# Order of the decode loads and steps: the first four value sequences before the last two key sequences, and three prompt units moved beside the last keys

## The chip, the cores and the metric

One core of one Trainium2 chip runs the whole program. The metric is the device time of the program in microseconds (us), as the median of several runs. The engines are TensorE (PE in the profile, its weight loads PEld), VectorE (DVE), ScalarE (ACT), GpSimd (POOL) and SyncE (SP), whose instruction queue issues nearly all DMA transfers.

## What is computed

A two-layer decoder step for a prompt of 256 tokens and for 8 sample sequences of 4 new tokens each. Layer 0 has a gated MLP mixer, layer 1 an attention mixer; each is followed by a mixture of experts with 16 experts. The change lies in the attention of layer 1, where the samples also read 1024 cached positions from 8 pages of 128 rows:

```
qs, ks_new, vs_new = attn_qkv(ns_in, pos_s, b_w_qkv[j], b_q_norm[j], b_k_norm[j])
past_k = cache_k[j][page_table].reshape(bs, past_len, N_KV_HEADS, HEAD_DIM)
past_v = cache_v[j][page_table].reshape(bs, past_len, N_KV_HEADS, HEAD_DIM)
k_all = jnp.concatenate([past_k, ks_new], axis=1)
v_all = jnp.concatenate([past_v, vs_new], axis=1)
os_ = moba_attention(qs, k_all, v_all, pos_s)
...
gate = jnp.where(fully_past[None, :, None, :], gate, NEG_INF)
_, sel = lax.top_k(gate, n_sel)
```

Each query takes the three best of four past blocks of 256 positions (by the sum of its scores against them), and its own block. There are 8 query heads and 4 key and value heads of 128; everything is float32.

## The kernel before

The kernel is written engine by engine: each engine has its own instruction list, and all order between engines is by semaphores. Nothing is scheduled by a planner; the order in the code is the order on the engine.

**The cached rows.** Each sample sequence b has keys K0 to K7 and values V0 to V7. One of them is 8 pages of 256 KB, 2 MB, which lie in a "home" in SBUF. The homes are the weight buffers of other stages: `c0` and `c1` (`ew_in`), `d` (`ew_down`), `b0` and `b1` (the halves of `half_b`), `a0` and `a1` (the halves of `half_a`). `K_HOME` and `V_HOME` say which home each takes. `sequence` on SP loads one: twice, it reads four page numbers into registers (L311) and issues four transfers (L313). Before most sequences SP waits until the home is free: on `sc`, which counts finished half sequences of keys (2 for each sequence), or on `pv`, which counts finished value sequences. At the end SP loads the output projection's weight w_o, 2 x 2 MB, into b0 and b1 (L333), and behind it prefetches experts' weights of the last stage.

**The attention loop.** Steps i = 0 to 17. In steps 0 to 15, step i turns four pages of keys (half a sequence): PE transposes each page into PSUM (L1311), DVE copies the even pages back (L970) and ACT the odd ones (L649). Step i also computes the scores of the half sequence before (`past_scores(i - 1)`, L1328). The prompt's attention is cut into 8 units (4 key heads x 2 chunks of 128 queries); one unit begins in each of steps 1 to 8 and ends in the next: scores (PE L1408), mask, maximum (DVE), exponent (ACT L696), normalising (DVE L1046), transposes (PE L1422), values (PE L1434), copy out (DVE L1051).

**The samples' softmax.** The 8 sequences form two groups of four. When the scores of a group are done, DVE takes sums and maxima (`past_stats`, L976), ranks the blocks and makes the bias (`past_bias`, L740 to L991), ACT takes exponents (`past_probs`, L658), DVE the sums (`past_sums`, L998), PE transposes the probabilities (`past_probs_up`, L1347), and PE multiplies them with the values: `past_values(b)` (L1370) for each cached sequence, `new_values(g)` (L1356) for the new tokens. ACT scales the result (`past_out`), PE transposes it (`past_rows`, L1379), DVE adds (L1019). Group 0's softmax lies in steps 8 to 10; all values come behind the loop. Then the output projection starts (L1097), which waits for both halves of w_o.

Of the kernel before, what the change touches and what calls it, by code (L numbers as in the profile page):

```python
# [12 lines left out]
P = 128  # L13
EPS = 1e-6
NEG = -1e30
KV = 4
# [37 lines left out]
def hybrid_step(nc, t, o):  # L54
# [29 lines left out]
    with ExitStack() as ctx:  # L84
# [28 lines left out]
        K_HOME = ("c0", "c1", "d", "b0", "b1", "a0", "a1", "c0")  # L113
        V_HOME = ("c1", "d", "b0", "b1", "a0", "a1", "c0", "c1")
# [9 lines left out]
        def landed(home, part, turn):  # L124
# [74 lines left out]
        Sn = sb("Sn", [P, TSA])  # L199
        Pn = sb("Pn", [P, TSA])  # L200
# [17 lines left out]
                 for x in (probT[:, :, :].rearrange("p s n -> p (s n)"), v_heads[:, 0:GRP * P])]  # L218
        q_all = v_heads[:, GRP * P:GRP * P + NG * P].rearrange("p (g a n) -> p g a n", g=NG, a=KV)
# [49 lines left out]
            kt kt_dve kt_act sc sn dbias dexp dnorm dpt dpt_act dpt_dve pv pv_sb new_v o_sb ot q_set  # L269
# [50 lines left out]
        SC_BANK = (6, 2)  # L320

# [9 lines left out]
        def _(sp):  # L331
# [112 lines left out]
            sp.wait_ge(S["sc"], 2)  # L444
            sequence(sp, 7, K_HOME[7], ck)
            for b in range(NB):


                if b < 7:
                    sp.wait_ge(S["sc"], 2 * (b + 2))  # L450
                else:
                    sp.wait_ge(S["pv"], 1)
                sequence(sp, b, V_HOME[b], cv)
            w_o = t["b_w_o"][0].rearrange("(k p) n -> p k n", p=P)
            for u in range(2):
                sp.wait_ge(S["pv"], 3 + u)
                load(w_o_at[u], w_o[:, :, u * HALF:(u + 1) * HALF], s_home[O_HOME[u]][0])
# [117 lines left out]
        def _(act):  # L575
# [75 lines left out]
            def past_probs(g):  # L651

                act.wait_ge(S["dbias"], g + 1)
                upto(act, S["dpt"], g)
                scores = PS[:, SC_BANK[g]:SC_BANK[g] + 2, :].rearrange("p a n -> p (a n)")
                for k in range(BLK):
                    w = slice(k * MOBA_BLOCK, (k + 1) * MOBA_BLOCK)
                    act.activation(Pd[:, w], scores[:, w], ACT.Exp, bias=dst[:, g, 16 + k:17 + k], scale=SCALE,  # L658
                                   accum_out=dst[:, g, 24 + k:25 + k]).then_inc(S["dexp"], 1)
                act.activation(Pn[:, :], Sn[:, :], ACT.Exp, bias=dst[:, g, 15:16], scale=SCALE,  # L660
                               accum_out=dst[:, g, 28:29]).then_inc(S["dexp"], 1)
# [13 lines left out]
            for i in range(NHF + 2):  # L675
# [6 lines left out]
                u = i - 2  # L682
                if 0 <= u < NU:
# [6 lines left out]
                u = i - 1  # L690
                if 0 <= u < NU:
                    w = (units[u][1] + 1) * P
                    act.wait_ge(S["pneg"], u + 1)
                    upto(act, S["pt"], u - 1)
                    for k in range(G):
                        last = act.activation(prob[:, u % 2, k * w:(k + 1) * w], PS[:, 2 + u % 2, k * w:(k + 1) * w], ACT.Exp,  # L696
                                              bias=stat[:, 1, u, k:k + 1], scale=SCALE, accum_out=stat[:, 2, u, k:k + 1])
                    last.then_inc(S["pexp"], 1)
                if i == PARTS + 1:
                    past_probs(0)  # L700
                if i == PARTS + 4:
                    past_probs_up(0)
            past_probs(1)
            past_out(0)
# [12 lines left out]
        def _(dve):  # L717
# [261 lines left out]
            def past_bias(g):  # L979

                ranks(link, dst[:, g, 0:4].unsqueeze(1), 1)
                link(dve.tensor_scalar(dst[:, g, 8:12], rank[:, 0, :], TOP_BLOCKS - 0.5, NEG, ALU.is_gt, ALU.mult))
                dve.tensor_tensor(dst[:, g, 4:8], dst[:, g, 4:8], dst[:, g, 8:12], ALU.add)
                dve.wait_ge(S["sn"], g + 1)
                upto(dve, S["dexp"], g * (BLK + 1))
                link(dve.tensor_tensor(Sn[:, :], PS[:, (5, 7)[g], 256:256 + TSA], own_neg[:, g * TSA:(g + 1) * TSA], ALU.add))
                dve.tensor_reduce(dst[:, g, 12:13], dst[:, g, 4:8], AX.X, ALU.max)
                link(dve.tensor_reduce(dst[:, g, 13:14], Sn[:, :], AX.X, ALU.max))
# [23 lines left out]
            def past_rows(g):  # L1012

                dve.wait_ge(S["ot"], g + 1)
                for bb in range(GRP):
                    past = PS[:, 4 + g, bb * P:(bb + 1) * P].rearrange("p (a b g t) -> p b a g t", a=KV, b=GRP, g=G)[:, bb]
# [5 lines left out]
            for i in range(NHF + 2):  # L1022
# [6 lines left out]
                u = i - 1  # L1029
                if 0 <= u < NU:  # L1030
                    c = units[u][1]
                    w = (c + 1) * P
                    both = PS[:, 2 + u % 2, 0:G * w].rearrange("p (g n) -> p g n", g=G)
# [8 lines left out]
                if 0 <= u < NU:  # L1042
# [4 lines left out]
                u = i - 2  # L1047
                if 0 <= u < NU:
# [3 lines left out]
                                    PS[:, 5, 0:G * P].rearrange("p (g n) -> p g n", g=G)).then_inc(S["po_sb"], 1)  # L1052
                if i == PARTS:
                    past_stats(0, 0)
                if i == PARTS + 1:
                    past_bias(0)
                if i == PARTS + 2:
                    past_sums(0)
                if i == PARTS + 4:
                    past_probs_up(0)  # L1060
                if i == PARTS + 5:
                    new_out(0)
                if i >= NHF:
                    past_stats(1, i - NHF)
# [4 lines left out]
            past_rows(0)  # L1069
# [14 lines left out]
        def _(pe):  # L1084
# [229 lines left out]
            def past_scores(hf):  # L1314
# [7 lines left out]
                if hf in (PARTS, PARTS + 1):  # L1322
                    pe.wait_ge(S["pexp"], NU - 1 + hf - PARTS)
# [14 lines left out]
            def past_probs_up(g):  # L1338

                if g == 0:  # L1340
                    pe.wait_ge(S["po_sb"], NU)
# [32 lines left out]
            def past_rows(g):  # L1374
                pe.wait_ge(S["o_sb"], g + 1)
                if g == 0:
                    pe.wait_ge(S["dpt_act"], 1)
                for bb in range(GRP):
                    mm = pe.transpose(PS[:, 4 + g, bb * P:(bb + 1) * P], o_rows[g][:, bb * P:(bb + 1) * P], ident)  # L1379
# [3 lines left out]
            for i in range(NHF + 2):  # L1383
# [15 lines left out]
                u = i - 1  # L1399
                if 0 <= u < NU:  # L1400
                    a, c = units[u]
                    w = (c + 1) * P
                    if u < 2:
                        pe.wait_ge(S["kvt_sb"], NT)
                        pe.wait_ge(S["vtok_sb"], 3 * NT)
                    upto(pe, S["pexp"], u - 1)
                    for k in range(G):
                        mm = pe.matmul(PS[:, 2 + u % 2, k * w:(k + 1) * w], zT[:, G * a + k, c * P:w], zT[:, NH + a, 0:w],  # L1408
# [5 lines left out]
                u = i - 2  # L1414
                if 0 <= u < NU:
# [11 lines left out]
                if 1 <= i <= NHF:  # L1427
                    past_scores(i - 1)
                if 0 <= u < NU:
# [7 lines left out]
                if i == PARTS + 4:  # L1437
                    past_probs_up(0)
                if i == PARTS + 5:
# [7 lines left out]
            past_rows(0)  # L1447
# [97 lines left out]
```

## Time and profile before

| what | value |
|---|---|
| median of 3 runs | 773.92 us (772.51 to 776.78) |
| the profiled execution's own time | 770.98 us |
| its span, first to last instruction | 769.1 us |
| PE busy | 628.2 us (82%) |
| DVE, ACT, POOL busy | 289.6, 157.2, 104.0 us |
| mean granted TensorE clock | 0.914 of full speed |
| DMA moved | 187.82 MB, mean 244 GB/s |
| attention loop to start of output projection | about 418 to 535 us of the span |

The span is what the trace covers; the profiled execution took 1.9 us more than it, and the median of the runs lies 2.9 us above that execution. A busy share over the whole span mixes stages with different limits; the rows further down are of the attention stage alone.

### The profile page before, as it was taken

The numbers are of one execution on the slowest core, as the hardware profiler recorded it, in microseconds if no ns is written. First come the engines' busy times: TensorE is split into PE (matmuls) and PEld (weight loads), VectorE is DVE, ScalarE is ACT, GpSimd is POOL, SyncE is SP. The second block draws the span as 40 slices with busy tenths as digits, with TensorE's granted clock in tenths as the row PEclk, the third lists the DMA queues.
The fourth block names the chain that finished last, engine by engine and source line by source line (L and its number), as shares of the span: only waits on it lengthen the run. The fifth ranks groups of instructions, "written<-read, shape, count | busy, mean of one in ns | idle before, by whom it ended". The sixth has DMA issues, their size and how long they took to land.

```text
span 769.1 us, 11977 instructions
## 1 busy us (share of the span) xinstructions
PE 628.2 (82%) x4067; PEld 430.0 (56%) x4067; DVE 289.6 (38%) x889; ACT 157.2 (20%) x326; POOL 104.0 (14%) x155
## 2 busy tenths in 40 slices
PE   5899999964899899279999997973987789898860
PEld 3677767732555555157667674662765456564430
DVE  2202121166334322244666775510027443334314
ACT  2115100020212221121112453211013113121210
POOL 0000000002222322000112000000000323322222
PEclk9999968995999999779999998995999799999995
DMA  9965030051997898599522774779923399699934
GB/s 343 290 266 219 22 150 1 0 212 37 381 410 296 330 412 354 173 386 319 170 95 95 237 245 144 244 222 360 404 80 148 131 401 411 239 406 414 409 138 174
DMA packets 65373, 187.82 MB, mean 244 GB/s; under 512 B 12044, under 2 KB 12606, under 8 KB 60982
## 3 DMA queue, kind: packets, MB, share of 16 engines
q1 hardware_dynamic: 58934, 175.50, 61.2%
q0 software_dynamic: 6400, 11.82, 4.2%
q8 instruction: 23, 0.38, 0.2%
q14 instruction: 16, 0.13, 0.1%
HBM read 182.95 MB, written 13.76 MB: 256 GB/s over the span
## 4 chain that ended last, share of the span: by engine, by line
PE 66%; DMA 10%; DVE 10%; SPq 5%; issue 5%; ACT 2%; DVEq 0%; POOLq 0%
PE PS L1097 26%; PE PS L1182 15%; PE PS L1200 7%; DMA ew_in<-in_moe_w_up 5%; PE PS L1088 3%; SPq L313 2%; SPq L311 2%; PE PS L1311 2%; DMA zT<-y_rows 2%; DMA half_b<-in_b_w_o 2%; PE PS L1268 2%; PE PS L1153 1%; PE PS L1113 1%; DVE zT L895 1%; PE PS L1265 1%
## 5 line engine op out<-in xcount | busy, mean ns | idle before, releaser
L1097 PE MATMUL PS<-hT,half_b 128*128 128x288 f32 x384 | 100.6, 422 | 10.4 <-DMA half_b<-in_b_w_o 7.1
L1182 PE MATMUL PS<-ew_in,zT 128*64 128x256 f32 x832 | 99.3, 392 | 6.3 <-DMA ew_in<-in_moe_w_up 3.1
L1097 PEld LDWEIGHTS PS<-hT,half_b 128*128 128x128 f32 x384 | 75.3, 197 | 34.4 <-issue 11.7
L1182 PEld LDWEIGHTS PS<-ew_in,zT 128*64 128x64 f32 x832 | 68.0, 142 | 45.3 <-issue 26.1
L895 DVE SCALAR_TENSOR_TENSOR zT<-PS,slot_gates,zT 64x256 f32<-64x256 f32 x34 | 16.5, 485 | 146.7 <-ACT zT L609 139.2
L1097 PE MATMUL PS<-hT,half_a 128*128 128x288 f32 x256 | 66.2, 417 | 3.1 <-DVE hT L725 3.1
L1200 PE MATMUL PS<-ew_down,zT 128*64 128x512 f32 x208 | 51.3, 611 | 14.5 <-issue 14.5
L1097 PEld LDWEIGHTS PS<-hT,half_a 128*128 128x128 f32 x256 | 49.0, 194 | 20.0 <-issue 4.1
L531 POOL DMA_INDIRECT y_rows<-zT,out_idx x34 | 34.3, 1010 | 149.4 <-ACT zT L612 149.4
L505 POOL DMA_INDIRECT zT<-h_rows,in_idx x38 | 39.8, 1046 | 50.3 <-PE PS L1162 18.7
L612 ACT COPY zT<-PS 128x512 f32<-128x512 f32 x34 | 19.9, 585 | 128.2 <-PE PS L1200 128.2
L511 POOL DMA_DIRECT2D h_rows<-tokbuf x2 | 1.7, 868 | 323.1 <-ACT tokbuf L600 323.1
L584 ACT ACTIVATE sq<-xT 128x288 f32<-128x288 f32 x32 | 13.6, 442 | 123.2 <-DVE xT L732 95.6
L578 ACT ACT_TABLE_LOAD x25 | 32.1, 1283 | 24.8 <-DVE pairs L867 23.7
L732 DVE TENSOR_TENSOR xT<-PS,xT 128x288 f32<-128x288 f32 x16 | 7.3, 458 | 70.5 <-PE PS L1097 70.5
L1097 PE MATMUL PS<-zT,half_a 128*128 128x288 f32 x128 | 33.4, 420 | 0.0
L1200 PEld LDWEIGHTS PS<-ew_down,zT 128*64 128x64 f32 x208 | 15.0, 137 | 30.7 <-issue 30.7
L723 DVE RECIPROCAL rec<-std 128x288 f32<-128x288 f32 x5 | 9.8, 1953 | 55.7 <-ACT std L588 55.7
L1162 PE MATMUL PS<-cst,zT 128*128 128x128 f32 x144 | 27.7, 316 | 3.1 <-DMA zT<-h_rows,in_idx 3.1
L609 ACT ACTIVATE zT<-PS 64x256 f32<-64x256 f32 x34 | 12.8, 377 | 83.1 <-PE PS L1182 83.1
L1097 PEld LDWEIGHTS PS<-zT,half_a 128*128 128x128 f32 x128 | 25.2, 198 | 7.2
L875 DVE COPY zT<-PS 128x512 f32<-128x512 f32 x36 | 24.9, 692 | 9.4 <-PE PS L1162 5.6
(258 smaller groups left out, 847.3 us busy)
## 6 DMA issues: line engine op xcount, KB each, us to landing
ew_in<-in_moe_w_gate SPq DMA_DIRECT2D x26, 1024.0 KB
ew_in<-in_moe_w_up SPq DMA_DIRECT2D x26, 1024.0 KB
ew_down<-in_moe_w_down SPq DMA_DIRECT2D x26, 1024.0 KB
ew_in<-in_cache_k SPq DMA_DIRECT2D x24, 256.0 KB, 4.8
ew_in<-in_cache_v SPq DMA_DIRECT2D x24, 256.0 KB, 3.4
half_a<-in_a_w_in SPq DMA_DIRECT2D x1, 4096.0 KB, 15.5
half_b<-in_a_w_in SPq DMA_DIRECT2D x1, 4096.0 KB, 25.8
half_a<-in_a_w_out SPq DMA_DIRECT2D x1, 4096.0 KB, 13.8
```

The source lines that it names most:

```text
L311: at = [eng.value_load(pages[0:1, bass.ds(b * NPAGE + j, 1)], min_val=0, max_val=NPOOL - 1) for j in pp]
L505: pool.indirect_dma_start(out=x_slots[:, u, :], out_offset=None, in_=h_dram.rearrange("t (h n) -> (t h) n", h=2), in_offset=bass.IndirectO ...
L531: pool.indirect_dma_start(out=y_dram[l].rearrange("t k (h n) -> (t k h) n", h=2), out_offset=bass.IndirectOffsetOnAxis(ap=out_idx[u][:, 0: ...
L578: act.activation(spare[:, :], eps[:, :], func)
L612: act.copy(y_slots[:, u, :], PS[:, 5 + u, :]).then_inc(E[l]["y_sb"], 1)
L875: dve.tensor_copy(x_slotsT[:, u], PS[:, u, :].rearrange("p (j h n) -> p j h n", j=4, h=2)).then_inc(el["xt_sb"], 1)
L895: dve.scalar_tensor_tensor(out=hid, in0=PS[SLOT:2 * SLOT, 2 + u, 0:EF], scalar=slot_gates[0:SLOT, 0, u:u + 1], in1=silu, op0=ALU.mult, op1 ...
L1088: mm = pe.matmul(PS[:, 7, 0:T], mean_d[:, :], sq[:, k, :], start=(k == 0), stop=(k == KT - 1))
L1097: mm = pe.matmul(PS[:, bank, 0:T], w[:, k, col:col + P], src[:, k, :], start=(k == 0), stop=(k == KT - 1))
L1162: mm = pe.transpose(PS[:, u, j * P:(j + 1) * P], x_slots[:, u, bass.ds(j, P, 4)], ident)
L1182: mm = pe.matmul(PS[f * SLOT:(f + 1) * SLOT, 2 + u, 0:EF], x_slotsT[:, u, k % 4, k // 4, :], w_in[u][:, f, k, :], start=(k == 0), stop=(k ...
L1200: mm = pe.matmul(PS[half * SLOT:(half + 1) * SLOT, 5 + u, :], hidT[:, f, :], w_down[u][:, f, half * HALF:(half + 1) * HALF], start=(f == 0 ...
```

## The change

SP loads K0 to K5 first, then V0 in the place where K6 stood, then V1, V2, V3, K6, K7, V4 to V7. The homes follow. K6 and K7 now lie in b0 and b1, so w_o waits for the scores of K6 and K7 (`sc` 14 and 16) instead of for values. The loop has one step fewer (0 to 16). In step 11 PE now does group 0's probabilities and all its values. The prompt units 0 to 4 stay in steps 1 to 5; units 5 to 7 begin in steps 13 to 15. `new_bias` takes the mask and maximum of the new tokens' scores out of `past_bias` and does them earlier. `Sn` and `Pn` move into free columns of `zT`.

```diff
-        K_HOME = ("c0", "c1", "d", "b0", "b1", "a0", "a1", "c0")
-        V_HOME = ("c1", "d", "b0", "b1", "a0", "a1", "c0", "c1")
+        K_HOME = ("c0", "c1", "d", "b0", "b1", "a0", "b0", "b1")
+        V_HOME = ("a1", "c0", "c1", "d", "a0", "a1", "c0", "c1")
...
+        PV_STEP = 11
+        EARLY = 5
+        def unit_at(i):
+            u = i - 1 if i <= EARLY else i - PV_STEP + EARLY - 2
+            return u if 0 <= u < (EARLY if i <= EARLY else NU) and (i <= EARLY or u >= EARLY) else None
+        def s_bank(u):
+            return (2 if u < EARLY else 6) + u % 2
...
-            for b in range(3, 7):
+            for b in range(3, 6):
                 sp.wait_ge(S["qkv"], 4 * (b - 2))
                 sequence(sp, b, K_HOME[b], ck)
+            sp.wait_ge(S["qkv"], 2 * KT)
+            sequence(sp, 0, V_HOME[0], cv)
...
-            sp.wait_ge(S["sc"], 2)
-            sequence(sp, 7, K_HOME[7], ck)
-            for b in range(NB):
-                if b < 7:
-                    sp.wait_ge(S["sc"], 2 * (b + 2))
-                else:
-                    sp.wait_ge(S["pv"], 1)
+            for b in range(1, 4):
+                sp.wait_ge(S["sc"], 2 * b)
+                sequence(sp, b, V_HOME[b], cv)
+            for b in range(6, 8):
+                sp.wait_ge(S["sc"], 2 * b - 4)
+                sequence(sp, b, K_HOME[b], ck)
+            sp.wait_ge(S["sc"], 12)
+            sequence(sp, 4, V_HOME[4], cv)
+            for b in range(5, NB):
+                sp.wait_ge(S["pv"], b - 4)
                 sequence(sp, b, V_HOME[b], cv)
             for u in range(2):
-                sp.wait_ge(S["pv"], 3 + u)
+                sp.wait_ge(S["sc"], 14 + 2 * u)
                 load(w_o_at[u], w_o[:, :, u * HALF:(u + 1) * HALF], s_home[O_HOME[u]][0])
...
+            def new_bias(g):
+                dve.wait_ge(S["sn"], g + 1)
+                link(dve.tensor_tensor(Sn[:, g, :], PS[:, (5, 7)[g], 256:256 + TSA], own_neg[:, g * TSA:(g + 1) * TSA], ALU.add))
+                dve.tensor_reduce(dst[:, g, 13:14], Sn[:, g, :], AX.X, ALU.max).then_inc(S["sn_sb"], 1)
...
+                    if u == EARLY:
+                        pe.wait_ge(S["sn_sb"], 2)
+                    if u in (EARLY, EARLY + 1):
+                        pe.wait_ge(S["o_sb"], 1)
...
+                    if u == EARLY:
+                        pe.wait_ge(S["pv_sb"], GRP)
...
-                if 1 <= i <= NHF:
+                if 1 <= i <= NHF and i != PV_STEP + 1:
                     past_scores(i - 1)
...
-                if i == PARTS + 4:
+                if i == PV_STEP:
                     past_probs_up(0)
-                if i == PARTS + 5:
+                    past_scores(i)
+                    past_values(0)
                     new_values(0)
-            for b in range(GRP - 1):
-                past_values(b)
+                    for b in range(1, GRP):
+                        past_values(b)
+                if i == PV_STEP + 1:
+                    past_rows(0)
             past_probs_up(1)
-            past_values(GRP - 1)
+            past_values(GRP)
             new_values(1)
-            past_values(GRP)
-            past_rows(0)
```

On PE, around group 0's softmax and step 11, the order before is this (L1311 turns key pages, L1328 scores, L1347 and L1348 transpose the probabilities, L1334 and L1356 are the new tokens' scores and values; one row may stand for many instructions):

```order
L1328 MATMUL PS<-half_b,zT 32x512 x4
L1311 MATMUL PS<-cst,half_a 128x128 x16
L1328 MATMUL PS<-half_a,zT 32x512 x4
L1311 MATMUL PS<-cst,half_a 128x128 x16
L1328 MATMUL PS<-half_a,zT 32x512 x4
L1347 MATMUL PS<-cst,shared 128x128 x8
L1348 MATMUL PS<-cst,Pn 32x128
L1311 MATMUL PS<-cst,half_a 128x128 x16
```

At the same place it now stands so (L1331 turns key pages, L1348 scores, L1367 and L1368 the probabilities, L1390 cached values, L1354 and L1376 the new tokens):

```order
L1348 MATMUL PS<-half_a,zT 32x512 x4
L1367 MATMUL PS<-cst,shared 128x128 x8
L1368 MATMUL PS<-cst,zT 32x128
L1348 MATMUL PS<-half_a,zT 32x512 x4
L1390 MATMUL PS<-half_a,ws_both 32x128 x32
L1354 MATMUL PS<-zT 32x32 x4
L1376 MATMUL PS<-PnT,tokbuf 128x32 x4
L1390 MATMUL PS<-ew_in,ws_both 32x128 x64
L1390 MATMUL PS<-ew_down,ws_both 32x128 x32
L1331 MATMUL PS<-cst,half_b 128x128 x16
```

Four value sequences (L1390) have moved ahead of the last four half sequences of keys.

On PE, behind the last key pages, the order before is this (L1370 cached values, L1379 transposes of the result):

```order
L1328 MATMUL PS<-ew_in,zT 32x512 x8
L1370 MATMUL PS<-ew_in,ws_both 32x128 x32
L1370 MATMUL PS<-ew_down,ws_both 32x128 x32
L1370 MATMUL PS<-half_b,ws_both 32x128 x32
L1347 MATMUL PS<-cst,shared 128x128 x8
L1348 MATMUL PS<-cst,Pn 32x128
L1370 MATMUL PS<-half_b,ws_both 32x128 x32
L1356 MATMUL PS<-PnT,tokbuf 128x32 x4
L1370 MATMUL PS<-half_a,sq 32x128 x32
L1379 MATMUL PS<-cst,shared 128x128 x4
```

There it now stands so (L1446 and L1458 are transposes and values of prompt unit 7):

```order
L1446 MATMUL PS<-cst,sq 128x128 x4
L1348 MATMUL PS<-half_b,zT 32x512 x4
L1458 MATMUL PS<-sq,tokbuf 128x256 x2
L1367 MATMUL PS<-cst,shared 128x128 x8
L1368 MATMUL PS<-cst,zT 32x128
L1390 MATMUL PS<-half_a,sq 32x128 x32
L1376 MATMUL PS<-PnT,tokbuf 128x32 x4
L1390 MATMUL PS<-half_a,sq 32x128 x32
L1390 MATMUL PS<-ew_in,sq 32x128 x64
L1397 MATMUL PS<-cst,shared 128x128 x4
```

Between the last scores and group 1's probabilities nothing of the values is left on PE; before, three value sequences stood there.

## Rows read from the trace of the kernel before

**Rows 1.** Chain that ended last, in order of time (start us, us, what).

```profile
475.21 0.27 SPq L311
...
520.75 0.43 SPq L333
521.23 14.03 DMA half_b<-in_b_w_o
...
554.56 3.88 PE PS L1097 x16
```

**Rows 2.** Waits of SP's queue, 432 to 521 (total us, times, longest).

```profile
SPq L311 <- PE PS L1328: 7.4, 3, 6.9
```

**Rows 3.** Timeline of SP's queue; last transfer of the new rows.

```profile
431.33 1.29 SPq L443 DMA_DIRECT2D out_vs<-tokbuf  x1
```

**Rows 4.** Timeline of PE, steps of the loop (start us, us, instruction).

```profile
446.24 1.04 PE L1311 MATMUL PS<-cst,half_b 128*128 128x128 f32 x8
...
450.70 1.04 PE L1311 MATMUL PS<-cst,half_b 128*128 128x128 f32 x8
...
466.44 1.04 PE L1311 MATMUL PS<-cst,half_a 128*128 128x128 f32 x8
...
472.16 1.12 PE L1311 MATMUL PS<-cst,half_a 128*128 128x128 f32 x4 [1.03 <-ACT half_a L649]
473.21 1.94 PE L1328 MATMUL PS<-half_b,zT 128*32 128x512 f32 x8
...
478.08 1.07 PE L1328 MATMUL PS<-half_a,zT 128*32 128x512 f32 x8
...
482.54 1.09 PE L1347 MATMUL PS<-cst,shared 128*128 128x128 f32 x8
...
488.39 1.09 PE L1311 MATMUL PS<-cst,ew_in 128*128 128x128 f32 x8
...
491.92 1.09 PE L1311 MATMUL PS<-cst,ew_in 128*128 128x128 f32 x8
```

**Rows 5.** Timeline of PE, the values behind the loop.

```profile
496.12 1.93 PE L1370 MATMUL PS<-ew_in,ws_both 128*32 128x128 f32 x64
497.87 1.93 PE L1370 MATMUL PS<-ew_down,ws_both 128*32 128x128 f32 x64
...
503.65 1.86 PE L1347 MATMUL PS<-cst,shared 128*128 128x128 f32 x8 [2.10 <-DVE Pn L998]
...
505.66 2.67 PE L1370 MATMUL PS<-half_b,ws_both 128*32 128x128 f32 x64
508.25 1.07 PE L1356 MATMUL PS<-PnT,tokbuf 32*128 32x32 f32 x8
...
527.15 1.11 PE L1379 MATMUL PS<-cst,shared 128*128 128x128 f32 x4 [0.81 <-ACT shared L671]
```

**Rows 6.** Timeline of DVE, the two groups' softmax and the last additions.

```profile
466.98 0.17 DVE L740 TENSOR_TENSOR cmp_ge<-dst 128x16 f32<-128x16 f32 x1
...
495.52 0.69 DVE L976 TENSOR_REDUCE dst<-PS 128x2 f32<-128x512 f32 x1 [0.77 <-PE PS L1328]
...
503.27 0.24 DVE L998 TENSOR_SCALAR Pn<-Pn,dst 128x32 f32<-128x32 f32 x1
...
528.30 0.48 DVE L1019 TENSOR_TENSOR hT<-PS,new_part 128x32 f32<-128x32 f32 x4 [15.55 <-PE PS L1379]
```

**Rows 7.** DMA issues of the page: size, median us from issue to landing.

```profile
ew_in<-in_cache_v SPq DMA_DIRECT2D x24, 256.0 KB, 3.4
```

**Rows 8.** Timeline of PE, first half of the output projection.

```profile
535.39 18.68 PE L1097 MATMUL PS<-hT,half_b 128*128 128x288 f32 x64 [7.12 <-DMA half_b<-in_b_w_o]
```

**Rows 9.** Stretches: us, busy of PE, PEld, DVE, ACT, POOL, granted clock, DMA share, GB/s.

```profile
484.00:496.00 12.00, 10.54 (x94) 6.68 (x96) 5.49 (x10) 3.88 (x7) 0.00 (x0) 1.00 0.72 242
...
503.60:505.70 2.10, 2.05 (x13) 1.67 (x16) 0.00 (x0) 0.00 (x0) 0.00 (x0) 0.54 0.67 224
...
558.00:571.50 13.50, 13.50 (x57) 10.58 (x56) 1.37 (x3) 1.33 (x3) 0.00 (x0) 1.00 0.00 1
```

More of the change, by code:

```diff
@@ L659, in past_probs @@
                                    accum_out=dst[:, g, 24 + k:25 + k]).then_inc(S["dexp"], 1)
-                act.activation(Pn[:, :], Sn[:, :], ACT.Exp, bias=dst[:, g, 15:16], scale=SCALE,
+                act.activation(Pn[:, :], Sn[:, g, :], ACT.Exp, bias=dst[:, g, 15:16], scale=SCALE,
                                accum_out=dst[:, g, 28:29]).then_inc(S["dexp"], 1)
@@ L674, in _ @@
             ready_for(ACT.Exp)
-            for i in range(NHF + 2):
+            for i in range(NHF + 1):
                 if i < NHF:
@@ L681, in _ @@
                         act.copy(vrow[0:n, c, :], PS[0:n, 2 + c, :]).then_inc(S["kvt_sb"], 1)
-                u = i - 2
-                if 0 <= u < NU:
+                u = unit_at(i - 1)
+                if u is not None:
                     w = G * (units[u][1] + 1) * P
@@ L689, in _ @@
                     key_page(4 * i + 3)
-                u = i - 1
-                if 0 <= u < NU:
+                u = unit_at(i)
+                if u is not None:
                     w = (units[u][1] + 1) * P
@@ L695, in _ @@
                     for k in range(G):
-                        last = act.activation(prob[:, u % 2, k * w:(k + 1) * w], PS[:, 2 + u % 2, k * w:(k + 1) * w], ACT.Exp,
+                        last = act.activation(prob[:, u % 2, k * w:(k + 1) * w], PS[:, s_bank(u), k * w:(k + 1) * w], ACT.Exp,
                                               bias=stat[:, 1, u, k:k + 1], scale=SCALE, accum_out=stat[:, 2, u, k:k + 1])
@@ L1020, in past_rows @@
                                       ALU.add).then_inc(S["pv_sb"], 1)
-            for i in range(NHF + 2):
+            for i in range(NHF + 1):
                 if i < NHF:
@@ L1028, in _ @@
                         dve.tensor_copy(ktok[0:n, c, :], PS[0:n, 2 + (NT + c) % 4, :]).then_inc(S["vtok_sb"], 1)
-                u = i - 1
-                if 0 <= u < NU:
+                u = unit_at(i)
+                if u is not None:
                     c = units[u][1]
                     w = (c + 1) * P
-                    both = PS[:, 2 + u % 2, 0:G * w].rearrange("p (g n) -> p g n", g=G)
+                    both = PS[:, s_bank(u), 0:G * w].rearrange("p (g n) -> p g n", g=G)
                     dve.wait_ge(S["ps"], u + 1)
@@ L1041, in _ @@
                     key_page(4 * i + 2)
-                if 0 <= u < NU:
+                if i == PARTS + 1:
+                    past_bias(0)
+                if u is not None:
                     rows2 = prob[:, u % 2, 0:G * w].rearrange("p (g n) -> p g n", g=G)
@@ L1046, in _ @@
                     dve.tensor_tensor(rows2, rows2, stat[:, 3, u, :].unsqueeze(2).to_broadcast([P, G, w]), ALU.mult).then_inc(S["pnorm"], 1)
-                u = i - 2
-                if 0 <= u < NU:
+                u = unit_at(i - 1)
+                if u is not None:
                     a, c = units[u]
@@ L1340, in past_probs_up @@
                 if g == 0:
[L1341 removed]
+                    pe.wait_ge(S["po_sb"], EARLY)
                 else:
@@ L1375, in past_rows @@
                 pe.wait_ge(S["o_sb"], g + 1)
-                if g == 0:
-                    pe.wait_ge(S["dpt_act"], 1)
                 for bb in range(GRP):
-                    mm = pe.transpose(PS[:, 4 + g, bb * P:(bb + 1) * P], o_rows[g][:, bb * P:(bb + 1) * P], ident)
+                    mm = pe.transpose(PS[:, (4, 1)[g], bb * P:(bb + 1) * P], o_rows[g][:, bb * P:(bb + 1) * P], ident)
                 mm.then_inc(S["ot"], 1)
             pe.wait_ge(S["qkv_sb"], 2 * KT - 2)
-            for i in range(NHF + 2):
+            for i in range(NHF + 1):
                 if i < NHF:
@@ L1398, in _ @@
                         mm.then_inc(S["kvt"], 1)
-                u = i - 1
-                if 0 <= u < NU:
+                u = unit_at(i)
+                if u is not None:
                     a, c = units[u]
@@ L1413, in _ @@
                     new_scores(0)
-                u = i - 2
-                if 0 <= u < NU:
+                u = unit_at(i - 1)
+                if u is not None:
                     c = units[u][1]
@@ L1426, in _ @@
                     key_page(4 * i + 3)
-                if 1 <= i <= NHF:
+                if 1 <= i <= NHF and i != PV_STEP + 1:
                     past_scores(i - 1)
-                if 0 <= u < NU:
+                if u is not None:
                     a = units[u][0]
```

40 lines of the change are left out of this document (19 added, 21 removed).

## Prediction

> **What bounds the stage now.** I read the chain in order of time first, since it says whose lateness ends the stage. From 475.21 to 520.75 it is nothing but SP's own instructions, register loads and transfer issues, then the transfer of w_o, which lands at 535.26 [rows 1]. PE stood idle for 7.12 us for it [rows 8]. So the attention stage ends 14.5 us after SP reaches w_o (535.26 - 520.75), and what SP does before sets that moment. The waits of SP come next: behind the new rows' transfers, which end at 432.62 [rows 3], it waited 7.4 us in all for scores, 6.9 of it in one piece [rows 2], and that piece ends at 475.21 [rows 1]. In the rest, 520.75 - 432.62 - 7.4 = 80.7 us, it issued nine sequences (K7, V0 to V7): **8.97 us each**. The mean DMA share is only 0.72 in such a stretch [rows 9], so it is the issuing, not the bandwidth, that has to be shortened or kept going. Last I read PE, DVE and ACT for the times at which they free the homes.
>
> **SP after the change.** K6's slot before the loop holds V0, a sequence for a sequence. After 432.62 nine remain: V1, V2, V3, K6, K7, V4, V5, V6, V7. Without waits they begin at 432.6, 441.6, 450.6, 459.5, 468.5, 477.5, 486.4, 495.4, 504.4, and w_o is reached at **513.35**. The gain from SP cannot exceed the 7.4 us of its waits. Now each release:
>
> Steps 0 to 5 are as before, but for new_bias(0) in step 3: two small DVE operations more, which no row prices alone there; like the chained one of [rows 6] at 0.17 us they are 0 to 0.4 us, and I take 0, since DVE waits for PE at the next page. Step 6 begins at 446.24 and with a unit lasts 4.46 us; a step with pages and scores alone lasts 3.53 [rows 4]. Step 6 still finishes unit 4: I take 3.8. Steps 7 and 8 have no unit: 446.24 + 3.8 + 2 x 3.53 = 457.1. Then `sc` 2 and 4 come as before (SP waited 0.5 us for both small waits together [rows 2]), `sc` 6 at about 449.7 and `sc` 8 at 457.1, each before SP comes for it (450.6 and 459.5).
>
> Group 0's softmax follows. Ahead of its bias stand, from step 9's begin: one page's transposes (half of 1.04 us [rows 4]), a page copy, two maxima and sums, another copy, all 128x512 on DVE like the 0.69 us row of [rows 6]; with starts that overlap a little I make it 3.2 us, an estimate. So the bias begins at 460.3 (before: 466.98 [rows 6]). PE will stall as before, since page 43 waits for an ACT copy queued behind ACT's exponents. From bias to the end of that step's scores was 473.21 + 1.94 - 466.98 = 8.2 us, half-speed scores included [rows 4, 6]. So `sc` 10 comes at **468.5**, before 475.15. SP wants it at 468.5 for K7: slack nil, and the one release that is tight. V4 wants `sc` 12: step 11's scores end 4.0 us later (479.15 - 475.15), the probabilities take 1.09, the next scores 1.07 [rows 4]: 474.7 against 477.5. V5 wants V0 done, 1.75 us on (497.87 - 496.12 [rows 5]): 476.5 against 486.4; V6 and V7 have more slack still, w_o wants `sc` 16, about 505 (below), against 513.4. So SP hardly waits, and w_o lands at 513.35 + 14.5 = **527.9**, 7.4 earlier.
>
> **PE after the change.** This chain had 7 us to spare and has it no more. From 474.7: V0 to V3 at 1.75, the new tokens' values at 1.07 [rows 5] and their few small scores, some 0.2: 8.3, to 483.0. Their data were issued by 459.5, 3.4 us from issue to landing each [rows 7]. Step 12 is 3.53 plus 1.2 for ACT's scaling and the transposes: 487.7. Step 13 has a unit's scores, 4.0; step 14 its transposes too, and they wait for DVE's additions of `past_rows(0)`, 5.5; step 15 like step 6 before, 4.46: 501.7. Step 16, without pages, waits for the last normalising and gives `sc` 16 and unit 7: 3.5, to 505.2, and DVE's copy of it 0.4. These five steps are the softest part of the sum; I allow 3 us either way.
>
> Then group 1's softmax, from the first maxima to the normalised Pn: 503.51 - 495.52 = 8.0 us [rows 6], to 513.6. Before, three value sequences covered it and PE waited 2.10 us [rows 5]; **now nothing covers it, and PE is idle for 8 us**. The probabilities take 2.0 (505.66 - 503.65) and two copies 0.9: 516.5. V4 at the slow 2.67, the new tokens 1.07 [rows 5], V5, V6, V7 at 1.75: 525.5. V7's last pages were issued before 513.4 and landed by 517, so PE no longer waits for them. Scaling, transposes and additions took 528.78 - 526.34 = 2.4 behind the last value sequence, PE having stopped 0.81 ahead of 527.15 [rows 5, 6]: hT is whole at **527.9**.
>
> So both ends meet; the projection starts near 528.0 instead of 535.39.
>
> **The clock of what follows.** The projection's first 64 matmuls took 18.68 us [rows 8], against 15.5 at full clock (4 x 3.88 [rows 1]): 3.1 us paid because PE came to them from 7.12 us of idling. After the change PE is busy from 513.6 on and idles 1 to 2 us. I take 2.0 of the 3.1, between nothing and all, nearer to all.
>
> The Trainium skill ("TensorE: Matmul & The Clock Gate", Part 1: The HAM clock gate) says that an idle TensorE falls to 1.2 GHz and that activity releases it to 2.4. The trace agrees in kind: the rows behind group 1's softmax show a granted clock of 0.54 [rows 9].
>
> **Later stages.** DMA is silent from 558 to 571.5 [rows 9], so the expert weights' prefetches have 13.5 us to spare. Some now wait for V5 to V7 on PE (about 522 to 525.5, before 521.94 and later, when w_o kept the engines full anyway). The experts' part follows the projection as before, and I move it whole. The moved tiles `Sn` and `Pn` cost nothing: same engines, same shapes.
>
> **Sum.** -7.4 - 2.0 = -9.4 us. Against the profiled execution: 770.98 - 9.4 = 761.6; against the median, 2.9 above that execution, 773.9 - 9.4 = **764.5 us**.
>
> **Rivals.**
> 1. PE's tail becomes the bound (chance 0.22). For it: the softmax without cover, and five steps that no row shows in this form. If they come 4 us later in all, the projection starts at 532, idle time before it vanishes and the clock gain is whole: -3.4 - 3.1, about 767.5. With 6 us it is 769.5. Against it: every piece has a row.
> 2. SP's idle time only moves (0.10). `sc` 10 has no slack: if group 0's softmax starts no earlier than DVE and ACT let it, say 4 us later than I reckon, K7 and all behind it come 4 us later, and the projection keeps a wait: -3.4 and no clock gain, 770.5. Against it: DVE and ACT lose three units' work in just these steps.
> 3. Slower (0.05). Steps 12 to 16, now with the probabilities and V4 to V7 all behind them, run at half clock, since much of what is in them is transposes and they stand between stalls. Their some 19 us of PE work and the tail would then grow by about 13: hT whole at 541, 5.6 us after the old start of the projection, and no clock gain: 779.5. It decides from 7.5 us of lateness on PE. Against it: pages and scores alone, 94 instructions of them in 484 to 496, ran at 1.00 [rows 9].
>
> The Trainium skill (same page, Part 4: PE-mode transpose) says that transposes do not count as busy for the clock. By that rule the loop of transposes would run at half speed and rival 3 would be likely. The trace disagrees: the row just named is mostly such transposes, and the granted clock is full, so the rule keeps only rival 3's small chance.
>
> The forecast itself has 0.63, with its own range of 761.5 to 767.5: the clock term 0 to 3.1, a landing of w_o up to 1.5 us quicker because the prefetches no longer follow at once, and the spread of the runs' medians.
>
> **Range and chances.** A measurement of this kernel tells some 0.5% (3.9 us) from no change. Faster needs under 770.05: forecast and nearly all of rival 1, and a third of rival 2: 0.87; same: the rest of those, 0.08; slower: 0.05. The range of 8 in 10 takes the forecast from 760.0 on (PE ready early, clock gain whole, w_o quicker) and rival 1 up to 770.0.
>
> **What would show it.** SP's waits for scores behind 432 fall from 7.4 to under 1.5 us; w_o is issued near 513; K7's release shows no or a short wait. PE has an idle gap near 8 us ahead of the transposes of group 1's probabilities, and no wait for cached values in the tail. The wait for w_o ahead of the projection falls from 7.12 us to under 2.5, and its first 64 matmuls from 18.68 to 15.5 to 17.5. The forecast is wrong if `sc` 10 comes after 471, if steps 13 to 16 take over 21 us, or if issuing a sequence takes longer than 8.97 us in the new order.

## The result, and the profile after

The changed kernel takes 770.26 us (median of 20 runs, 766.17 to 775.62) against 773.97 (20 runs): ratio 0.9948, 95% interval 0.9929 to 0.9967. That ratio stands for 4.0 us less, where 9.4 were forecast; the time lies 0.3 us above the forecast range of 760.0 to 770.0. A second set of runs of the same kernel gave 0.9932 (0.9908 to 0.9955). The mechanism was right in its first half, and only a size was off in the second: SP was freed as reckoned, but PE's tail ran almost 5 us longer than its sum.

First the waits of SP's queue from 431 to 540 (total us, times, longest), in answer to [rows 2]:

```profile
SPq L344 <- PE PS L1390: 11.0, 3, 9.2
```

No wait for scores is left. The 11.0 us are waits of the prefetches behind w_o, which hold up nobody. SP's timeline, in answer to [rows 1, 3]:

```profile
430.83 1.25 SPq L456 DMA_DIRECT2D out_vs<-tokbuf  x1
...
514.06 1.28 SPq L344 DMA_DIRECT2D half_b<-in_b_w_o  x2
```

w_o is issued at 514.06 (forecast 513.35, before 520.75). Nine sequences took 514.06 - 432.08 = 82.0 us, 9.1 each (forecast 8.97). The landing of its two halves (us, shortest, median, longest, from the transfers that read `in_b_w_o`):

```profile
DMA to landing us min/median/max: 11.4/13.9/16.3
```

The longest is the second half, issued at 514.5: w_o was whole at 530.8, not 527.9. Then PE's timeline, in answer to [rows 4, 5, 8]:

```profile
470.50 1.07 PE L1348 MATMUL PS<-half_a,zT 128*32 128x512 f32 x8
...
473.72 1.95 PE L1390 MATMUL PS<-half_a,ws_both 128*32 128x128 f32 x64
...
512.19 1.94 PE L1367 MATMUL PS<-cst,shared 128*128 128x128 f32 x8 [8.30 <-DVE zT L1015]
...
515.36 3.64 PE L1390 MATMUL PS<-half_a,sq 128*32 128x128 f32 x64 [1.02 <-ACT sq L680]
518.93 1.91 PE L1376 MATMUL PS<-PnT,tokbuf 32*128 32x32 f32 x8
520.77 3.60 PE L1390 MATMUL PS<-half_a,sq 128*32 128x128 f32 x61
...
529.32 0.85 PE L1390 MATMUL PS<-ew_in,sq 128*32 128x128 f32 x22 [1.91 <-issue]
530.98 1.11 PE L1397 MATMUL PS<-cst,shared 128*128 128x128 f32 x4 [0.80 <-ACT shared L685]
532.74 18.29 PE L1117 MATMUL PS<-hT,half_b 128*128 128x288 f32 x64 [0.65 <-DVE hT L1036]
```

In these rows x counts records: a float32 matmul leaves two, a transpose one. V4's 32 matmuls are x64, and the "first 64 matmuls" of the projection, here and in the prediction, are 64 records of 32 matmuls.

The eleventh half sequence of scores (`sc` 11) ends at 471.57 (forecast 472.5), V0 begins at 473.72 (forecast 474.7), the probabilities of group 1 begin at 512.19 (forecast 513.6). What comes behind them is slow: V4 takes 3.64 us, the new tokens 1.91, and there is a gap of 1.91 in the midst of V7. The projection starts at 532.74, and it is released by DVE's additions, no longer by w_o. The granted clock goes with most of it (us, busy of PE, PEld, DVE, ACT, POOL, clock, DMA share, GB/s):

```profile
503.80:512.20 8.40, 0.10 (x2) 0.04 (x1) 5.37 (x20) 2.23 (x10) 0.00 (x0) 0.70 0.80 249
...
515.30:519.00 3.70, 3.64 (x65) 3.29 (x65) 0.00 (x0) 0.00 (x0) 0.00 (x0) 0.50 0.91 270
...
520.80:524.20 3.40, 3.40 (x65) 3.12 (x68) 0.29 (x1) 0.00 (x0) 0.00 (x0) 0.50 1.04 397
524.20:527.40 3.20, 3.20 (x114) 2.94 (x105) 0.00 (x0) 0.00 (x0) 0.00 (x0) 1.00 1.06 393
...
532.70:536.00 3.30, 3.26 (x7) 2.41 (x8) 0.00 (x0) 0.00 (x0) 0.00 (x0) 0.50 1.04 418
```

The clock fell to half while PE idled for 8.3 us, and stayed there until 524.2, twelve microseconds after PE's work had begun again. It fell once more around the short idle times ahead of the projection.

The profiled execution took 770.5 us, only 0.5 below the one of before, which was 3 us under its own median. The projection is 2.65 us ahead of before; the first expert matmuls are at 601.01 here and at 602.75 before, 1.7 ahead. Most of what goes on the way there goes in 24 transposes ahead of the experts, which took 5.38 us at a granted clock of 0.50 and took 4.31 before. Of the rest, 0.6 goes at the very end, where the last gather of rows took 7.90 us against 7.30. One profile can't settle 1 or 2 us after the attention; the runs' ratios do.

### The profile page after: what moved, and what is told of

It is laid out like the page before. It is cut to its first block, busy times and chain, and to the rows that moved or that the text cites. A ratio compares the mean times of both kernels' runs of the same rounds, so it can differ in the third digit from the quotient of the medians.

```text
span 768.6 us, 11977 instructions
## 1 busy us (share of the span) xinstructions
PE 632.9 (82%) x4067; PEld 433.4 (56%) x4067; DVE 289.9 (38%) x889; ACT 157.4 (20%) x326; POOL 104.0 (14%) x155
## 4 chain that ended last, share of the span: by engine, by line
PE 70%; DVE 11%; DMA 10%; issue 4%; ACT 3%; SPq 1%; DVEq 0%; POOLq 0%; ACTq 0%
PE PS L1117 26%; PE PS L1202 14%; PE PS L1220 7%; DMA ew_in<-in_moe_w_up 6%; PE PS L1331 3%; PE PS L1108 3%; PE PS L1390 2%; DMA zT<-y_rows 2%; PE PS L1288 2%; PE PS L1348 1%; PE PS L1133 1%; PE PS L1173 1%; SPq L344 1%; DVE zT L910 1%; PE PS L1285 1%
## 5 line engine op out<-in xcount | busy, mean ns | idle before, releaser
L1220 PE MATMUL PS<-ew_down,zT 128*64 128x512 f32 x208 | 51.3, 611 | 14.5 <-issue 14.5
## 6 DMA issues: line engine op xcount, KB each, us to landing
half_a<-in_a_w_in SPq DMA_DIRECT2D x1, 4096.0 KB, 15.4
```

Source lines behind the costliest of these rows:

```text
L1220: mm = pe.matmul(PS[half * SLOT:(half + 1) * SLOT, 5 + u, :], hidT[:, f, :], w_down[u][:, f, half * HALF:(half + 1) * HALF], start=(f == 0 ...
```

## The experiments

Two theories of the shortfall stood against each other. A: PE's tail sets the end now, and is long because PE comes to it from idling. B: the tail is held up by what feeds it (V4 to V7, copies), or w_o still sets the end. All ratios are to the kernel before, with their 95% intervals.

**1. Fill the softmax gap with 14 matmuls** (extra work, result unused).

```diff
+            for _ in range(14):
+                pe.matmul(PS[:, 4, :], ident, cst[:, 0:HALF], start=True, stop=True)
             past_probs_up(1)
             past_values(GRP)
```

> The changed kernel with 14 extra matmuls (128x512, result unused, into a free PSUM bank) on PE between the last scores and the transposes of group 1's probabilities. They take 6.8 us of the 8.3 us in which PE is idle there. Theory A (the tail is late because PE comes to it from 8.3 us of idling and then runs at half clock from 512.2 to 524.2): the clock is full, the transposes still begin near 512, the tail from there to the projection shrinks from 20.5 to about 14 us (V4 1.8 us instead of 3.6, new values 1.0 instead of 1.8), the projection then waits for w_o, which lands near 528.5, and its first 64 matmuls take 15.5 to 17 us: 4 to 6 us faster than the changed kernel, ratio to the kernel before 0.987 to 0.990. Theory B (the tail is late because it is fed by something else, V4 to V7's transfers or the copies on ACT and DVE): the tail stays 20 us long, the time stays at 770.

Measured: 0.9919 (0.9893 to 0.9946), 768.21 us. PE's timeline of this run:

```profile
505.18 12.18 PE L1471 MATMUL PS<-cst 128*128 128x512 f32 x28
517.20 1.04 PE L1367 MATMUL PS<-cst,shared 128*128 128x128 f32 x8
...
519.36 1.95 PE L1390 MATMUL PS<-half_a,sq 128*32 128x128 f32 x64 [1.02 <-ACT sq L680]
...
527.39 1.72 PE L1390 MATMUL PS<-ew_in,sq 128*32 128x128 f32 x50 [1.01 <-issue]
...
532.34 17.45 PE L1117 MATMUL PS<-hT,half_b 128*128 128x288 f32 x64 [1.80 <-DMA half_b<-in_b_w_o]
```

I had put the matmuls at half their price: they took 12.2 us, not 6.8 (0.87 each, two records each), and held the probabilities up to 517.20. All the same V4 takes 1.95 and the new tokens 1.07, from the probabilities to the projection it is 15.1 us instead of 20.5, and PE waits for w_o at its end. Theory B's tail would have stayed at 20. It is also plain that w_o is close behind: it landed at 532.3. The time fell by 1 to 2 us against the changed kernel, not by 4 to 6, and the intervals overlap.

**2. All prompt units early** (`EARLY = 8`).

```diff
-        EARLY = 5
+        EARLY = 8
```

> The changed kernel with all eight prompt units back in steps 1 to 8 (EARLY = 8); the order of loads and of values stays. Theory A (PE's tail sets the end, SP is no longer the bound): steps 13 to 16 get about 4.5 us shorter, but steps 6 to 8 get 3 us longer, so the third and fourth releases and group 0's softmax come 5 to 6 us later and SP waits some 5 us again; PE's order of work is then as long as before, the tail ends within 2 us of the changed kernel's, w_o lands near 534: time 770 to 774. Rival (the moved units are what costs the tail, and SP has time to spare): 766 to 768, 3 us faster than the changed kernel.

Measured: 0.9965 (0.9936 to 0.9995), 772.24 us. SP's waits, and PE:

```profile
SPq L311 <- PE PS L1348: 5.0, 3, 3.7
```

```profile
476.46 1.95 PE L1390 MATMUL PS<-half_a,ws_both 128*32 128x128 f32 x64
...
507.60 1.94 PE L1367 MATMUL PS<-cst,shared 128*128 128x128 f32 x8 [7.14 <-DVE zT L1015]
...
525.42 0.66 PE L1397 MATMUL PS<-cst,shared 128*128 128x128 f32 x4 [0.79 <-ACT shared L685]
...
533.46 17.35 PE L1117 MATMUL PS<-hT,half_b 128*128 128x288 f32 x64 [7.38 <-DMA half_b<-in_b_w_o]
```

The time is as theory A expected, and so is SP: 5 us of its waits are back, w_o is issued at 515.67, lands at 533.3, and the projection waits 7.38 us for it. But PE's tail ended 5.6 us earlier than in the changed kernel (525.42 against 530.98 for the transposes of the result), not within 2: V0 began 2.7 us later (476.46 against 473.72), as expected, but what follows it up to the probabilities was 7.3 us shorter, not 4.5. So each part has its price: late units buy SP's time with PE's.

**3. w_o ahead of V7.**

```diff
-            for b in range(5, NB):
+            for b in range(5, NB - 1):
                 sp.wait_ge(S["pv"], b - 4)
                 sequence(sp, b, V_HOME[b], cv)
...
                 load(w_o_at[u], w_o[:, :, u * HALF:(u + 1) * HALF], s_home[O_HOME[u]][0])
+            sp.wait_ge(S["pv"], 3)
+            sequence(sp, NB - 1, V_HOME[NB - 1], cv)
```

> The changed kernel with w_o's two transfers issued ahead of V7 on SP instead of behind it. Theory A (PE's tail sets the start of the projection, w_o lands some 4 us before it): w_o is early by 9 us and nothing is gained, V7 lands about 10 us later than now, near 526 to 527 instead of 517, which PE wants at 524: 0 to 3 us slower. Rival (w_o still sets the start, as forecast): 4 us faster or more.

Measured: 0.9927 (0.9896 to 0.9958), 767.43 us; its interval overlaps those of the changed kernel (0.9948 and 0.9932). Its profiled execution took 766.57 us. PE:

```profile
515.14 3.64 PE L1392 MATMUL PS<-half_a,sq 128*32 128x128 f32 x64 [1.02 <-ACT sq L682]
...
523.79 3.67 PE L1392 MATMUL PS<-ew_in,sq 128*32 128x128 f32 x128
528.27 0.66 PE L1399 MATMUL PS<-cst,shared 128*128 128x128 f32 x4 [0.82 <-ACT shared L687]
529.58 15.79 PE L1119 MATMUL PS<-hT,half_b 128*128 128x288 f32 x64 [0.65 <-DVE hT L1038]
```

The tail starts as slow as in the changed kernel, so w_o's place does not touch the clock there. But the gap in the midst of V7 is gone, and the projection starts 3.2 us earlier than in the changed kernel and runs at full clock. Both expectations missed: not slower, and the 3 us come from another source than w_o's landing, since PE never waited for w_o in the changed kernel either.

**4. The kernel before, with 8 matmuls ahead of its wait for w_o.**

```diff
             pe.wait_ge(S["pv_sb"], NG * GRP)
+            for _ in range(8):
+                pe.matmul(PS[:, 4, :], ident, cst[:, 0:HALF], start=True, stop=True)
```

> The kernel before with 8 extra matmuls (128x512, result unused) on PE ahead of its wait for w_o, where it idles 7.1 us. If idling ahead of the projection is what makes its first 64 matmuls take 18.7 instead of 15.5 us: they take 15.5 to 17 us and the whole is 2 to 3 us faster, ratio 0.996 to 0.997. If the clock there is set by something else: no difference. 8 matmuls take 3.9 us at full and 7.8 us at half clock, so at worst they delay the projection by 1 us.

Measured: 0.9997 (0.997 to 1.0025). PE:

```profile
528.30 8.52 PE L1453 MATMUL PS<-cst 128*128 128x512 f32 x16 [0.57 <-DVE hT L1019]
536.66 15.74 PE L1097 MATMUL PS<-hT,half_b 128*128 128x288 f32 x64
...
575.00 5.74 PE L1113 MATMUL PS<-hT,w_route 128*20 128x288 f32 x16 [3.20 <-DVE hT L725]
```

The first 64 matmuls take 15.74 instead of 18.68, so the idling ahead of them is what costs them their clock, and this part ends 1.7 us earlier. But nothing arrives: the routing matmuls behind it take 5.74 us, where the kernel before has

```profile
576.67 4.06 PE L1113 MATMUL PS<-hT,w_route 128*20 128x288 f32 x16 [3.20 <-DVE hT L725]
```

and both end at 580.7 (575.00 + 5.74, 576.67 + 4.06). The clock's gain ahead of the projection was given back two steps later. In the profiles of all kernels here the routing matmuls took 5.6 to 5.75 us wherever the projection's first 64 took 17.45 or less, and 4.06 where these took 17.89 or more (before, changed, experiments 5 and 7). Why the one goes with the other no run shows. The forecast's clock term was worth little in time even where it could be had.

**5. Fill the gap with 8 matmuls**, as 1 with `range(8)`.

> The changed kernel with 8 extra matmuls in PE's softmax gap instead of 14 (14 took 12.2 us, 0.87 each, and held the probabilities up by 4 us; 8 take 7.0 of the 8.3 us). If the half clock after the gap is what lengthens the tail: probabilities begin at 512 to 513, the tail to the projection shrinks from 20.5 to 13 us, hT is whole near 526, and w_o, which landed at 530.8 in the changed kernel's profile and at 532.3 in the one with 14, is then the bound: projection at 530 to 532, PE idle 4 to 6 us for it. 1 to 3 us faster than the changed kernel, 767 to 769. If w_o's landing were no bound, 764.

Measured: 0.9925 (0.99 to 0.995), 768.65 us. PE:

```profile
503.57 7.03 PE L1471 MATMUL PS<-cst 128*128 128x512 f32 x16
512.04 1.06 PE L1367 MATMUL PS<-cst,shared 128*128 128x128 f32 x8 [1.44 <-DVE zT L1015]
...
514.23 1.95 PE L1390 MATMUL PS<-half_a,sq 128*32 128x128 f32 x64 [1.02 <-ACT sq L680]
...
523.42 1.29 PE L1390 MATMUL PS<-ew_in,sq 128*32 128x128 f32 x38 [1.75 <-issue]
525.51 0.66 PE L1397 MATMUL PS<-cst,shared 128*128 128x128 f32 x4 [0.80 <-ACT shared L685]
529.69 17.89 PE L1117 MATMUL PS<-hT,half_b 128*128 128x288 f32 x64 [3.53 <-DMA half_b<-in_b_w_o]
```

As expected, and the cleanest evidence for theory A: the same work from 512 on is through 5.5 us earlier (525.51 against 530.98), and the only change is a busy PE ahead of it. Then w_o is the bound, PE idles 3.53 us for it (4 to 6 expected), and the clock falls again. The time itself is 0.7 and 1.6 us under the changed kernel's two medians, which is within the noise: what the filling does is shown in the rows of the tail, not in the time.

**6. 8 matmuls, and w_o ahead of V7** (3 and 5 together).

> The 8 extra matmuls and w_o issued ahead of V7. Both bounds are gone: w_o lands near 519, the tail runs at full clock, V7 lands near 522 and is what PE may wait for. Projection near 525 at full clock (first 64 matmuls 15.5 to 16): 10 us earlier than before and 3 us of clock, time 761 to 764, ratio 0.983 to 0.987. If only the one bound mattered (w_o), it is no faster than with w_o moved alone, 767.

Measured: 0.9939 (0.9913 to 0.9966), 770.61 us. PE:

```profile
516.66 3.59 PE L1392 MATMUL PS<-half_a,sq 128*32 128x128 f32 x64 [1.01 <-ACT sq L682]
...
522.95 1.93 PE L1392 MATMUL PS<-ew_in,sq 128*32 128x128 f32 x64
526.42 1.26 PE L1392 MATMUL PS<-ew_in,sq 128*32 128x128 f32 x32 [1.53 <-DMA ew_in<-in_cache_v]
529.47 1.08 PE L1392 MATMUL PS<-ew_in,sq 128*32 128x128 f32 x32 [1.79 <-DMA ew_in<-in_cache_v]
```

A clear miss. Behind 4 MB of w_o, V7 lands late (its second half near 529), so V7 takes w_o's place as the bound. I had put its landing at 522. The filling also did less here than in experiment 5: V4 took 3.59 us, at a granted clock of 0.53, with the same 8 matmuls in the gap and the same 1.44 us of idling behind them. So the 8 matmuls make a full clock in the tail likely (experiments 5, 7 and 10 have it), not certain; why it fell here is open.

**7. As 6, with seven units early** (`EARLY = 7`).

> As the last, with seven prompt units in steps 1 to 7 and one beside the last keys (EARLY = 7). With w_o ahead of V7 the release of w_o no longer hangs on SP's waits, so the later releases may cost less: PE's steps 13 to 16 lose two units (some 2 to 3 us), but K7 and V4 to V7 come 2 to 4 us later and V7 is then the last to land. Between 2 us faster and 2 us slower than with five early units; faster would show that PE's own length is the bound, slower that V7's landing is.

Measured: 0.9975 (0.9954 to 0.9996), 773.33 us. PE:

```profile
529.36 1.94 PE L1392 MATMUL PS<-ew_in,sq 128*32 128x128 f32 x32 [5.64 <-DMA ew_in<-in_cache_v]
```

2.7 us slower than experiment 6, though the intervals still touch (0.9954 to 0.9996 against 0.9913 to 0.9966): SP waits for scores again, 4.5 us in two waits, and V7 comes later yet. That speaks for keeping three units late; experiment 2, with none of them late, points the same way.

**8. The changed kernel once more.**

> The changed kernel once more, unaltered, for its spread from profile to profile. If the slow stretches of the first profile were bad luck, they are gone: tail 14 us. If they belong to the order: PE idle 8.3 us ahead of the probabilities, half clock for most of the next 12 us, tail about 20 us, w_o landing at 530 to 532 and the projection at 531 to 534; time 769 to 771.

Measured: 0.9932 (0.9908 to 0.9955), 769.32 us. PE:

```profile
514.19 1.94 PE L1367 MATMUL PS<-cst,shared 128*128 128x128 f32 x8 [8.31 <-DVE zT L1015]
...
517.35 3.64 PE L1390 MATMUL PS<-half_a,sq 128*32 128x128 f32 x64 [1.01 <-ACT sq L680]
```

Idle time, half clock, a gap (0.81 us here) in the midst of V7, projection at 533.18: the slow tail belongs to the order of the work. The two profiles of this kernel differ by 2.0 us in when the tail begins (512.19, 514.19), so a difference between the start times of two runs is good to about 2 us; lengths within one profile tell more.

**9. w_o spread:** its first half ahead of V6, its second ahead of V7.

```diff
             for b in range(5, NB):
+                if b >= 6:
+                    u = b - 6
+                    sp.wait_ge(S["sc"], 14 + 2 * u)
+                    load(w_o_at[u], w_o[:, :, u * HALF:(u + 1) * HALF], s_home[O_HOME[u]][0])
                 sp.wait_ge(S["pv"], b - 4)
                 sequence(sp, b, V_HOME[b], cv)
```

> The changed kernel with w_o's first half issued ahead of V6 and its second ahead of V7, each where SP comes to it after its release (scores of K6 near 494, of K7 near 503). w_o then moves in bandwidth that the page loads leave unused and no longer holds up V7 for 10 us. If PE's tail at half clock is the bound: w_o lands near 515, V7 near 521, PE waits for neither, projection at 528 to 530 as with w_o ahead of V7, time 766 to 768. If bytes at the end still were the bound: as the changed kernel, 770.

Measured: 0.9898 (0.9876 to 0.992), 765.73 us. PE, and two stretches of the windows:

```profile
514.51 3.64 PE L1391 MATMUL PS<-half_a,sq 128*32 128x128 f32 x64 [1.01 <-ACT sq L681]
...
523.19 3.67 PE L1391 MATMUL PS<-ew_in,sq 128*32 128x128 f32 x128
527.68 0.66 PE L1398 MATMUL PS<-cst,shared 128*128 128x128 f32 x4 [0.82 <-ACT shared L686]
528.98 15.79 PE L1118 MATMUL PS<-hT,half_b 128*128 128x288 f32 x64 [0.65 <-DVE hT L1037]
```

```profile
504.00:508.00 4.00, 0.00 (x0) 0.00 (x0) 3.65 (x15) 0.00 (x0) 0.00 (x0) 0.75 1.06 389
...
520.00:524.00 4.00, 4.00 (x96) 3.77 (x100) 0.29 (x1) 0.00 (x0) 0.00 (x0) 0.62 0.01 4
```

As expected. The DMA engines are full ahead of the tail (389 GB/s, against 249 in the changed kernel's gap) and empty from 520 to 524, V7 has no gap, PE waits for no transfer. The interval lies clear of the changed kernel's first (0.9929 to 0.9967) and overlaps its second (0.9908 to 0.9955); there are 6 runs of this one.

**10. w_o spread, and the 8 matmuls** (5 and 9 together).

> The same with the 8 extra matmuls in PE's softmax gap. If the two bounds are PE's clock in the tail and the landing of w_o and V7, this removes both: tail 13 us, projection at 524 to 526 at full clock, time 760 to 764. If it is not under 766, a further bound stands there that I have not named.

Measured: **0.9862 (0.9839 to 0.9885), 764.12 us**, the lowest median of all. PE:

```profile
515.46 1.95 PE L1391 MATMUL PS<-half_a,sq 128*32 128x128 f32 x64 [1.01 <-ACT sq L681]
...
524.21 1.29 PE L1391 MATMUL PS<-ew_in,sq 128*32 128x128 f32 x38 [1.30 <-issue]
526.30 0.66 PE L1398 MATMUL PS<-cst,shared 128*128 128x128 f32 x4 [0.80 <-ACT shared L686]
527.60 15.79 PE L1118 MATMUL PS<-hT,half_b 128*128 128x288 f32 x64 [0.65 <-DVE hT L1037]
```

The tail takes 14.3 us (513.28 to 527.60), no transfer is waited for, and the projection starts 5.1 us earlier than in the changed kernel. The tail was expected to take 13 and the projection to start by 526; the time is at the edge of what was expected. Its interval lies clear of both kernels'. From experiment 9 it is not quite clear (the intervals overlap by 0.0009, with 6 runs of each), so that eight useless matmuls save time on top of the spreading is likely, and shown only in the length of the tail: 14.3 us against 17.6 (511.34 to 528.98).

## Why the prediction was wrong

**SP: right.** The bound of before, the ceiling of 7.4 us and the releases came out as worked out: `sc` 10 came at 467.3 (forecast 468.5, wrong from 471), no wait for K7 though its slack was nil, w_o issued 0.7 us later than forecast. One of the three signs of a wrong forecast did come true, a sequence took 9.1 us to issue and not 8.97, but it cost 1.3 us over nine of them and not the forecast. Experiment 2, which takes three units back, shows SP's waits at 5.0 us and the projection waiting for w_o as before.

**Steps 6 to 16 of PE: right.** The probabilities of group 1 began 1.4 us earlier than forecast, the idle time ahead of them was 8.3 us where 8 was said. Steps 13 to 16 took 17.5 us as forecast, at a granted clock of 1.00 (484 to 496), so rival 3 did not come. The row that the prediction set against rival 3 shows transposes mixed with score matmuls, though. It does not tell what transposes do alone: the 24 ahead of the experts ran at 0.50 for all of their 5.4 us in the changed kernel.

**The tail's size: the step that failed.** The prediction had named the uncovered softmax, and then took "V4 at the slow 2.67, the new tokens 1.07, V5, V6, V7 at 1.75". The 2.67 was the price after 2.10 us of idling [rows 5]; after 8.3 us the clock stayed at half for all of V4, the new tokens and V5. From V4's start to V7's end it is 14.85 us (515.36 to 530.21), not 9.0: 1.91 of the difference is the gap in V7, 3.9 the clock. With the start 1.1 earlier than forecast, hT was whole 4.8 late (532.7 against 527.9), so the sum's -7.4 came out as -2.65 in the profile. Experiment 5 ends the same stretch 5.5 us earlier by keeping PE busy ahead of it. This was rival 1, which put the projection at 532 for 4 us of lateness. It named the uncovered softmax and soft steps as the reasons, not the clock of the tail, and it counted on the whole clock gain behind it, which did not come.

**w_o's landing: off by 2.9 us.** I took 14.5 us from SP's reaching w_o; 0.7 of the 2.9 is the later issue. Its second half took 14.0 us in the kernel before, and 16.3, 16.1, 17.2, 16.1, 15.4 and 15.8 wherever it stood behind V7 later (experiments 4 and 5 among them; 4 is the kernel before in all its loads). The forecast rested on one profile, which had a short one; what makes the landing vary was not tested. In the changed kernel it is hidden by the tail, by 1.9 us; with the tail cured it is the bound (experiments 1, 5). Against the changed kernel, by the ratios, curing the tail alone gained some 1 to 2 us (within the noise), spreading w_o alone some 3 to 4 (no gap in V7 and a projection at full clock, experiment 9), both together 5 to 7.

**The clock term: 2.0 us forecast, 0.4 measured.** The idle times ahead of the projection were short, as forecast, but there were three of them (1.91, 0.80, 0.65), and the clock was at half again when it began. And experiment 4 shows what such a gain is worth: of 2.9 us, 1.3 went into a later start and 1.7 back to the routing stage. The later start need not be the extra matmuls' doing: they ended at 536.8, and w_o landed at 536.5 in that profile, 16.1 us after the issue of its second half.

**Later stages "moved whole": true only within about 2 us.** Of 2.65 us of lead at the projection, the profile shows 3.0 at the routing matmuls (573.63 against 576.67) and 1.7 at the first expert matmuls.

**The range** was too narrow at the top: both ends of the stage had been priced from one row each, and each from a fast sample; they were taken together as if "the ends meet" made the sum safe, where of two bounds the later one counts.

What stays open: the gap in the midst of V7 (1.91, 1.01, 0.95, 1.75, 0.81, 1.30 us in the changed kernel and experiments 1, 2, 5, 8 and 10). PE has a semaphore to wait for only at the start of each half of V7, records 65 and 97 of the 128 that V6 and V7 leave together. The gap lies elsewhere, and it keeps to one place in PE's instruction list: behind record 106 or 107 without extra matmuls, behind record 90 with 8 of them ahead (16 records more), behind record 78 with 14 (28 more). In each of the six, one packet of 0.02 MB of a DMA queue that the profile calls "instruction" moved in the last 2 us ahead of the gap, with the DMA share at 0.97 to 1.06 in the 4 us around it. In experiments 3 and 9, which have no gap, it moved over 3 us before PE came to that place, and the engines were less busy (a share of 0.46 from 523.0 to 523.5 in 3, 0.01 from 520 to 524 in 9). That PE's instructions are fetched late behind full DMA engines would fit all of this; no experiment was made that tests it.

Open too is why the clock needed 12 us to come back in the tail, and only a few behind other idle times.

## What to carry to other kernels

When work is moved away from under a wait, price not only the wait but what runs after it. Here PE idled 8 us and did its next 12 us at half clock, and the row after a 2 us wait didn't tell that price. The price isn't a fixed one either: behind 7.12 us of idling the projection's first part lost 3 us and no more. Where two chains end within a microsecond of each other, the gain is that of the slower sample of the later one; mend both before judging either. A large load that competes with a stream limited by its issuing belongs into the stream's gaps as soon as its place is free, not behind it: here that was worth 0.3 to 0.5% on top of the change's own 0.5 to 0.7% (0.9898 against 0.9948 and 0.9932).

## What the runs showed of the hardware

- TensorE's granted clock stayed at 0.50 for 12 us (512.2 to 524.2, PE busy for 11.0 of them) after 8.3 us of idling, and so it did in experiments 2 (after 7.14 us), 3, 8 and 9, to within 0.5 us. After 2.10 us of idling it was 0.54 to begin with and full within 5 us.
- Behind 7.12 us of idling the projection's matmuls, 128x288 with 128x128 weights, lost only 3.1 us to the clock (18.68 against 15.5), and 1.8 behind 7.38 us in experiment 2. So the length of the idle time alone does not say how long the half clock lasts.
- A 128x512 float32 matmul with a 128x128 weight took 0.87 us at full clock (14 in 12.18 us). Four 128x512 score matmuls with 32-column weights took 1.07 us together; each record of one lasts about 0.6 us, so they run side by side.
- The clock gained at one place was paid at the next: 15.74 against 18.68 us for the projection's first part, then 5.74 against 4.06 for the routing, with both kernels level at 580.7 (experiment 4).
- The same 2 MB load, the second half of w_o behind the same work, took 14.0 us to land in the kernel before and 16.1 in experiment 4, which has the same order of loads.
